# GLA level products of a diffusion block in column groups of 32 and 64 instead of full 128x128 matmuls

## The chip, the cores and the metric

The kernel runs on one core of a Trainium2 chip. The metric is the device time of one execution in microseconds (us). Engines: TensorE (PE; its weight loads are listed as PEld), VectorE (DVE), ScalarE (ACT), GpSimd (POOL) and SyncE (SP), which issues most DMAs.

## The reference

The block takes 256 latent tokens of width 2048 and 256 context tokens. After an RMSNorm with modulation comes one large projection, then two branches, retention and gated linear attention (GLA), each of 4 heads; their outputs are gated, merged and projected; a SwiGLU layer follows. What the change touches is the GLA branch, here for one head, in both directions:

```python
b = jnp.cumsum(ac, axis=2)                       # log decay, one per key channel (128)
decay = jnp.exp(b[:, :, :, None, :] - b[:, :, None, :, :])   # where i >= j (backward: the other half, exclusive)
scores = jnp.einsum('bhid,bhjd,bhijd->bhij', qc, kc, decay)
o = einsum('bhij,bhjv->bhiv', scores, vc) + einsum('bhid,bhdv->bhiv', qc * exp(b), s)
```

The decay depends on the query i, the key j and the channel d, so the 256x256 scores of a head are not one matmul. They have to be built for all pairs of tokens.

## The kernel before, in words

**Large matmuls.** Every weight block of 512 columns is streamed from HBM into `raw` (8 buffers), split by ScalarE into a rounded part `w_hi` (L643) and by VectorE into the rest `w_lo` (L1045), and multiplied by TensorE in three products for each pair of 128 rows (`products`, L1619, L1623, L1631): 12 float32r matmuls of 128x128 weights and 512 columns in a slot. ScalarE may split a slot only once TensorE has used the one four before it. This stream goes on through the whole kernel.

**The heads.** While TensorE computes the later columns of the input projection, the two branches are computed head by head between its slots. There is no planner: each engine has a list written out by hand, with a place p from 0 to 15 for each head. On TensorE `at_head(i, p)` (L1833) comes after the product slot of place p; on ScalarE and VectorE the steps of place p come before the split of that place. Each engine's list is in order, and semaphores tie them together.

**GLA scores by levels.** For a level h of 1, 2, 4, ..., 128, tokens are cut into blocks of 2h. A query in one half of a block and a key in the other half are compared through the middle of that block, so that the decay is a product of a query part and a key part. `exponents` (L1210) writes the two parts of the exponents for one level, for all 256 tokens, into `g_arg` (128 channels, 2, 4 levels, 256 tokens); ScalarE takes the exponential of four levels at once (L844); `weigh` (L1253) multiplies by queries and keys. Then TensorE multiplies keys by queries over the 128 channels (L1867): for levels 1 to 64 two 128x128 products, one for each half of 128 tokens; for level 128 two products that cross the halves. Levels 1, 2, 4, 8 are multiplied at p = 4, levels 16, 32, 64, 128 at p = 8, into banks 6 and 7 of PSUM. Of a 128x128 product only the pairs that belong to the level are wanted.

**Picking.** `g_a[:, 0:2, :]` starts as a diagonal matrix with the sum of q times k of each token (L1298). `pick` (L1261) then merges one level after another with a masked copy (L1273, 128 partitions by 256 elements, mask of 128x128 for each level), each waiting for the one before it. Near levels are picked at p = 5, ahead of the exponents of levels 16 to 128; far levels at p = 10. ScalarE copies the cross products of level 128 (L862). At p = 10 TensorE multiplies `g_a` by the values (L1887 to L1890).

**Beside it** the retention branch runs: transposes of its keys and queries at p = 3 and 6 (L1853, L1878), ScalarE's copies of them, behind the exponential of g_arg on its list (L856 r_qt, L858 r_kt), scores at p = 7 (L1896), the weighting by VectorE (L1309), outputs at p = 9 (L1912). GpSimd turns queries and keys by their position and issues the loads of the next head.

**A block of column groups** exists already elsewhere: L1801 sums 16 pieces of 512 columns with 32 columns of ones as weights, each in one of four groups of 32 columns of the array.

Of the kernel before, what the change touches and what calls it, by code (L numbers as in the profile page):

```python
# [10 lines left out]
U8 = mybir.dt.uint8  # L11
# [4 lines left out]
P = 128  # L16
D = 2048
KT = D // P
L = 256
# [30 lines left out]
def constants():  # L50

    f = np.float32
    n_f = RDK // 4
    inv = (f(10000.0) ** (-np.arange(n_f, dtype=f) / f(n_f))).astype(f)
    t = np.arange(L)
    ang = np.concatenate([(t // 64).astype(f)[:, None] * inv, (t % 64).astype(f)[:, None] * inv], axis=-1)
    rope = np.stack([np.cos(ang), np.sin(ang)], axis=1).astype(f)
    rope = rope.reshape(MT, P, 2, P).transpose(1, 2, 0, 3)
    s = np.arange(L)[:, None]
    i = np.arange(L)[None, :]  # L60
    delta = i - s
    dist = np.stack([np.maximum(delta, 0), np.maximum(-delta, 0), i + L - s, L - i + s], axis=0).astype(f)
    dist = dist.reshape(4, MT, P, L).transpose(2, 0, 1, 3)
    a, b = np.arange(P)[:, None], np.arange(P)[None, :]
    mask = np.stack([((a // h != b // h) & (a // (2 * h) == b // (2 * h))) for h in LEVELS[:-1]], axis=1)
    return {"k_ident": np.eye(P, dtype=f), "k_rope": np.ascontiguousarray(rope),
            "k_dist": np.ascontiguousarray(dist),
            "k_mask": np.ascontiguousarray(mask.astype(f))}


def build(nc, x, c, ctx_in, c_ctx, w_mod, b_mod, norm_mix_pre, norm_mix_post, norm_ffn_pre, norm_ffn_post,
# [10 lines left out]
    with ExitStack() as ctx:  # L82
# [5 lines left out]
        def keep(name, shape, dt=F32):  # L88

            size = math.prod(shape[1:]) * (4 if dt != mybir.dt.uint8 else 1)  # L90
            off = cursor[0]
            cursor[0] += (size + 31) // 32 * 32
            return at(name, shape, dt, off)
# [3 lines left out]
        def S(name):  # L97
            if name not in sems:
                sems[name] = ctx.enter_context(nc.semaphore(name))
            return sems[name]  # L100
# [21 lines left out]
        scale1 = keep("scale1", [P, 2, KT])  # L122
        mod2 = keep("mod2", [P, 2, KT])
        lg = keep("lg", [P, 2 * RH])
        mask = keep("mask", [P, 7, P], U8)
        spare = keep("spare", [P, 16])
        ssq = keep("ssq", [P, 4])
        rstd = keep("rstd", [P, 4])
# [11 lines left out]
        def reg(name, shape, kb, dt=F32):  # L140

            return at(name, shape, dt, base + kb * K)
# [4 lines left out]
        acc = reg("acc", [P, 4, D], 0)  # L147
        hc_hi = reg("hc_hi", [P, KT, L], 32, F32R)
        hc_lo = reg("hc_lo", [P, KT, L], 48, F32R)
        mask_f = reg("mask_f", [P, 7, P], 88)  # L150
        rows2 = reg("rows2", [96, P], 92)
        junk0 = reg("junk0", [P, D], 32)
        mod_row = reg("mod_row", [P, MOD_BLOCKS, N], 64)
# [277 lines left out]
        def _(pool):  # L431
# [15 lines left out]
            pool.dma_start(mask_f[:, :, :], k_mask).then_inc(S("consts_landed"), 16)  # L447
            pool.dma_start(ga_w[:, :, :], w_in_k[:, :, C_GA:C_GA + 2 * LOW]).then_inc(S("ga_landed"), 16)
            pool.dma_start(rope[:, :, :, :], k_rope).then_inc(S("tables_landed"), 16)
            pool.wait_ge(S("mask_ready"), 1)  # L450
            pool.memset(al_t[0][:, :], 1.0).then_inc(S("gate_rows_set"), 1)
            for r in (0, 64):
                for d in range(2):
# [585 lines left out]
        def _(dve):  # L1039
# [97 lines left out]
            for b in range(1, CTX_BLOCKS):  # L1137
                if b == 2:
                    dve.wait_ge(S("consts_landed"), 16 * 5)
                    dve.tensor_copy(mask[:, :, :], mask_f[:, :, :]).then_inc(S("mask_ready"), 1)  # L1140
                for j in range(8):
                    for n in chunks_at(b, j, 0):
                        add_chunk(0, n, *chunk_of(n))
                    split(S_CTX + 8 * b, j)
                    for n in chunks_at(b, j, 1):
                        add_chunk(0, n, *chunk_of(n))
# [102 lines left out]
            def hold(n):  # L1249

                dve.memset(spare[:, n:n + 1], 0.0)
# [6 lines left out]
                                             g_qkt[:, a:a + 1, :].broadcast_to([P, 4, L]), ALU.mult)  # L1258
                last.then_inc(S("g_qk_ready"), 1)

            def pick(i, r, n):  # L1261

                dve.wait_ge(S("g_levels_done"), i * 2 + (r + 1))
                if r == 1:
                    dve.wait_ge(S("g_cross_ready"), i + 1)
                for e in range(n):
                    if r == 1 or e > 0:
                        dve.wait_ge(S("g_picked"), i * 7 + (4 * r + e))
                    else:
                        dve.wait_ge(S("g_diag_ready"), i + 1)  # L1270
                    hold(4 * r + e)
                    src = bank(6, 2)[:, e * L:(e + 1) * L].rearrange("p (a n) -> p a n", a=2)
                    dve.copy_predicated(g_a[:, 0:2, :],  # L1273
                                        mask[:, 4 * r + e:4 * r + e + 1, :].broadcast_to([P, 2, P]), src)\
                        .then_inc(S("g_picked"), 1)

            dve.wait_ge(S("dctx_ready"), RH)
# [1 line left out]
            def head(i, final):  # L1279

                for p in range(16):
# [3 lines left out]
                    if p == 3:  # L1285
                        dve.wait_ge(S("g_st_exp"), i * 2 + 2)
                        dve.tensor_tensor(g_st[:, :, :], g_st[:, :, :], g_qkt[:, 0:1, :].broadcast_to([P, 2, L]), ALU.mult)\
                            .then_inc(S("g_st_ready"), 1)
                        dve.wait_ge(S("g_qk_landed"), i * 32 + 32)
                        dve.tensor_tensor(g_a[:, 0:2, :], g_q[:, :, :], g_k[:, :, :], ALU.mult)\  # L1290
                            .then_inc(S("g_diag_summed"), 1)
                        dve.wait_ge(S("g_diag_summed"), i * 2 + 1)
                        dve.tensor_reduce(spare[:, 12:12 + MT], g_a[:, 0:2, :], AX_X, ALU.add)\
                            .then_inc(S("g_diag_summed"), 1)
                        dve.wait_ge(S("g_diag_summed"), i * 2 + 2)
                        hold(9)
                        for m in range(MT):
                            last = dve.tensor_scalar(g_a[:, m, :], ident[:, :], spare[:, 12 + m:13 + m], GDK ** -0.5,  # L1298
                                                     ALU.mult, ALU.mult)
                        last.then_inc(S("g_diag_ready"), 1)  # L1300
                    if p == 5:
                        pick(i, 0, 4)
                        for e in range(4):
                            exponents(i, 4 + e)
                    if p == 7:
# [4 lines left out]
                                          dmat[:, bass.ds(i, 1), :, :].rearrange("p o a n -> p (o a) n"), ALU.mult)\  # L1310
                            .then_inc(S("r_a_ready"), 1)
                    if p == 10:
                        pick(i, 1, 3)

                        dve.wait_ge(S("r_o_done"), i + 1)
                        for m in range(MT):
                            dve.bn_stats(stats[:, 0, m, :], bank(4)[:, m * RDK:(m + 1) * RDK]).then_inc(S("r_stat"), 1)
                        dve.wait_ge(S("r_stat"), i * 4 + 2)
                        hold(8)
                        for m in range(MT):  # L1320
                            dve.bn_aggr(mv[:, 0, m, :], stats[:, 0, m, :]).then_inc(S("r_stat"), 1)
                        dve.wait_ge(S("r_stat"), i * 4 + 4)
                        dve.tensor_scalar(mv[:, 0, :, 1:2], mv[:, 0, :, 1:2], EPS, None, ALU.add)\
                            .then_inc(S("r_var_ready"), 1)
# [280 lines left out]
        def _(pe):  # L1605
# [227 lines left out]
            def at_head(i, p):  # L1833
# [15 lines left out]
                if p == 3:  # L1849
# [3 lines left out]
                            last = pe.transpose(bank(4)[:, f * L + m * P:f * L + (m + 1) * P],  # L1853
                                                r_kc[:, m, f * P:(f + 1) * P], ident[:, :])
                    last.then_inc(S("r_kc_turned"), 1)
                if p in (4, 8):
                    r = (p - 4) // 4
                    pe.wait_ge(S("g_qk_ready"), i * 2 + (r + 1))
                    if r == 0:
                        pe.wait_ge(S("g_s_ready"), i + 1)  # L1860
                    else:
                        pe.wait_ge(S("g_picked"), i * 7 + 4)
                    for e in range(4):
                        for m in range(MT):
                            key = m
                            qry = m if 4 * r + e < 7 else 1 - m
                            last = pe.matmul(bank(6, 2)[:, e * L + m * P:e * L + (m + 1) * P],  # L1867
                                             g_arg[:, 1, e, key * P:(key + 1) * P], g_arg[:, 0, e, qry * P:(qry + 1) * P],
                                             start=True, stop=True)
                    last.then_inc(S("g_levels_done"), 1)  # L1870
                if p == 6:
                    pe.wait_ge(S("rope_ready"), i * 4 + 4)
# [6 lines left out]
                                                    t[:, m, f * P:(f + 1) * P], ident[:, :])  # L1879
                    last.then_inc(S("r_qk_turned"), 1)  # L1880
                if p == 10:
                    pe.wait_ge(S("g_picked"), i * 7 + 7)
                    pe.wait_ge(S("g_cross_ready"), i + 1)
                    pe.wait_ge(S("g_st_ready"), i + 1)
                    for m in range(MT):
                        o, c = bank(6)[:, m * GDV:(m + 1) * GDV], slice(m * P, (m + 1) * P)
                        pe.matmul(o, g_a[:, m, :], g_v[:, 2 + m, :], start=True, stop=False)  # L1887
                        pe.matmul(o, g_a[:, 3 - m, :], g_v[:, 3 - m, :], start=False, stop=False)
                        pe.matmul(o, g_st[:, 0, c], g_s[:, 0, :], start=False, stop=False)
                        last = pe.matmul(o, g_st[:, 1, c], g_s[:, 1, :], start=False, stop=True)  # L1890
                    last.then_inc(S("g_o_done"), 1)
# [225 lines left out]
```

## Time and profile before

| | |
|---|---|
| median of 3 runs | 1728.86 us (1727.52 to 1730.07) |
| the profiled execution: time, span | 1727.43 us, 1725.7 us |
| TensorE busy | 1697.5 us, 98% |
| VectorE busy | 1010.8 us, 59% |
| ScalarE busy | 740.0 us, 43% |
| heads | from about 542 to 800 us |

The span is the time from the first to the last instruction of one profiled execution. Busy is the time in which an engine executed at least one instruction. A float32 matmul appears as two records of weight load and two of stream, a float32r matmul or a transpose as one of each. Streams are pipelined, so a record's length (275 ns for 128 columns) is more than the step from one to the next (109 ns).

### The profile page before, as it was taken

How to read it: one execution, taken by the hardware profiler on the slowest of the kernel's cores; microseconds unless marked ns; L12 is line 12 of the kernel's file. 1: busy time of each engine (PE TensorE's matmuls, PEld its weight loads, DVE VectorE, ACT ScalarE, POOL GpSimd, SP SyncE). 2: the span in 40 equal slices, each digit the busy share in tenths (PEclk: the TensorE clock that was granted, in tenths of full speed). 3: DMA queues.
4: the chain of work that ended last, by engine and by line, in shares of the span. 5: the costliest groups of instructions: out<-in, count | busy, mean ns of one | idle time of the engine just before them, and what ended most of it. 6: DMA issues, size and time to landing. Idle time of an engine off the chain costs nothing.

```text
span 1725.7 us, 21272 instructions
## 1 busy us (share of the span) xinstructions
PE 1697.5 (98%) x7805; PEld 1371.5 (79%) x7805; DVE 1010.8 (59%) x1145; ACT 740.0 (43%) x832; POOL 161.3 (9%) x179
## 2 busy tenths in 40 slices
PE   6999999999999999999999999999999999999998
PEld 2468888887878888888888788888888888888886
DVE  2446776648966677666665764444444545444444
ACT  3334222217555354455446564444444444443442
POOL 0011000000046245230000000000000000000000
PEclk9999999999999999999999999999999999999999
DMA  9999999968988666656776566666666666766652
GB/s 366 378 382 379 352 370 342 364 252 309 380 291 266 190 217 188 209 157 208 230 250 229 192 210 192 187 190 187 190 189 189 188 189 191 260 194 195 193 193 91
DMA packets 183708, 419.69 MB, mean 243 GB/s; under 512 B 12961, under 2 KB 13313, under 8 KB 173793
## 3 DMA queue, kind: packets, MB, share of 16 engines
q1 hardware_dynamic: 167680, 375.45, 65.7%
q0 software_dynamic: 7216, 28.07, 5.0%
q10 hardware_dynamic: 8752, 15.38, 2.4%
q8 instruction: 38, 0.62, 0.1%
q14 instruction: 22, 0.17, 0.0%
HBM read 398.35 MB, written 20.50 MB: 243 GB/s over the span
## 4 chain that ended last, share of the span: by engine, by line
PE 94%; DVE 2%; DMA 2%; issue 1%; ACT 1%; SPq 0%; POOL 0%; DVEq 0%; POOLq 0%; ACTq 0%
PE ps L1619 27%; PE ps L1623 27%; PE ps L1631 27%; PE ps L1701 2%; PE ps L1675 2%; DMA raw<-in_w_mod 2%; PE ps L1717 1%; PE ps L1896 1%; PE ps L1912 1%; PE ps L1950 1%; PE ps L1867 1%; PE ps L2028 0%; PE ps L1664 0%; PE ps L2015 0%; PE ps L2020 0%
## 5 line engine op out<-in xcount | busy, mean ns | idle before, releaser
L1045 DVE TENSOR_TENSOR w_lo<-raw,w_hi 128x1024 fp32r<-128x1024 f32 x486 | 600.5, 1238 | 509.2 <-ACT w_hi L643 508.9
L643 ACT ACTIVATE w_hi<-raw 128x1024 fp32r<-128x1024 f32 x488 | 515.9, 1060 | 781.1 <-PE ps L1631 764.7
L1619 PE MATMUL ps<-w_hi,h_hi 128*128 128x512 f32 x1440 | 452.7, 395 | 0.0
L1623 PE MATMUL ps<-w_hi,h_lo 128*128 128x512 f32 x1440 | 445.3, 390 | 0.0
L1631 PE MATMUL ps<-w_lo,h_hi 128*128 128x512 f32 x1440 | 392.6, 389 | 0.0
L1623 PEld LDWEIGHTS ps<-w_hi,h_lo 128*128 128x128 f32 x1440 | 270.4, 188 | 56.7
L1631 PEld LDWEIGHTS ps<-w_lo,h_hi 128*128 128x128 f32 x1440 | 270.3, 188 | 56.3
L1619 PEld LDWEIGHTS ps<-w_hi,h_hi 128*128 128x128 f32 x1440 | 266.9, 188 | 55.1 <-ACT w_hi L643 1.5
L1057 DVE SCALAR_TENSOR_TENSOR acc<-wm,csil,acc 128x2048 f32<-128x2048 f32 x60 | 140.9, 2349 | 57.8 <-DMA wm<-in_w_mod 57.6
L1619 PE MATMUL ps<-w_hi,hid_hi 128*128 128x512 f32 x352 | 109.8, 390 | 0.0
L1623 PE MATMUL ps<-w_hi,hid_lo 128*128 128x512 f32 x352 | 109.7, 389 | 0.0
L1631 PE MATMUL ps<-w_lo,hid_hi 128*128 128x512 f32 x352 | 94.8, 389 | 0.0
L1631 PEld LDWEIGHTS ps<-w_lo,hid_hi 128*128 128x128 f32 x352 | 66.1, 188 | 13.7
L1623 PEld LDWEIGHTS ps<-w_hi,hid_lo 128*128 128x128 f32 x352 | 66.1, 188 | 13.7
L1619 PEld LDWEIGHTS ps<-w_hi,hid_hi 128*128 128x128 f32 x352 | 66.0, 188 | 13.6
L1623 PE MATMUL ps<-w_hi,hc_lo 128*128 128x512 f32 x192 | 59.1, 389 | 0.0
L1619 PE MATMUL ps<-w_hi,hc_hi 128*128 128x512 f32 x192 | 59.1, 389 | 0.0
L1631 PE MATMUL ps<-w_lo,hc_hi 128*128 128x512 f32 x192 | 57.8, 389 | 0.0
L1675 PE MATMUL ps<-raw,c_pad 128*32 128x512 f32 x256 | 45.3, 617 | 8.1 <-DMA raw<-in_w_mod 6.2
L623 POOL DMA_DIRECT2D hs<-hsd x1 | 0.7, 718 | 479.1 <-DVE hid_n L1565 479.1
L1107 DVE TENSOR_TENSOR w_lo<-raw,w_hi 128x1024 fp32r<-128x1024 f32 x16 | 19.3, 1223 | 44.3 <-ACT w_hi L716 44.3
L1623 PEld LDWEIGHTS ps<-w_hi,hc_lo 128*128 128x128 f32 x192 | 36.1, 188 | 7.5
(308 smaller groups left out, 1407.4 us busy)
## 6 DMA issues: line engine op xcount, KB each, us to landing
raw<-in_w_in SPq DMA_DIRECT2D x184, 512.0 KB, 6.3
wm<-in_w_mod SPq DMA_DIRECT2D x64, 1024.0 KB, 7.0
raw<-in_ffn_w_gate SPq DMA_DIRECT2D x88, 512.0 KB, 4.5
raw<-in_ffn_w_up SPq DMA_DIRECT2D x88, 512.0 KB, 4.4
raw<-in_ffn_w_down SPq DMA_DIRECT2D x88, 512.0 KB, 4.6
raw<-in_w_mod SPq DMA_DIRECT2D x64, 512.0 KB, 8.1
raw<-in_w_out SPq DMA_DIRECT2D x32, 512.0 KB, 4.7
px<-stage ACTq DMA_DIRECT2D x44, 256.0 KB, 6.0
```

The costliest lines, as they stand in the source:

```text
L643: act.activation(w_hi[:, j % SPLIT, :, :], raw[:, j % RAW, :, :], ACT.Copy).then_inc(w_high, 1)
L1045: dve.tensor_tensor(w_lo[:, j % SPLIT, :, :], raw[:, j % RAW, :, :], w_hi[:, j % SPLIT, :, :].bitcast(F32), ALU.subtract).then_inc(w_low, 1)
L1057: dve.scalar_tensor_tensor(out=a, in0=wm[:, b, :], scalar=csil[:, k:k + 1], in1=a, op0=ALU.mult, op1=ALU.add).then_inc(S("wm_used"), 1)
L1107: dve.tensor_tensor(w_lo[:, o % SPLIT, :, :], raw[:, place % RAW, :, :], w_hi[:, o % SPLIT, :, :].bitcast(F32), ALU.subtract)\
L1619: pe.matmul(o, hi[:, kk, c], w_h[:, e, :], start=kk == 0, stop=False)
L1623: pe.matmul(o, lo[:, kk, c], w_h[:, e, :], start=False, stop=False)
L1631: last = pe.matmul(o, hi[:, kk, c], w_l[:, e, :], start=False, stop=kk == last_k)
L1675: last = pe.matmul(bank(6)[g * GROUP:(g + 1) * GROUP, :], c_pad[:, k, :], raw[:, place % RAW, e, :], start=k < 4, stop=k >= KT - 4, tile_p ...
L1701: last = pe.matmul(bank(n), t[:, 2 * i + e, m * P:(m + 1) * P], w[:, q, e, :], start=i == 0 and r == 0 and a == 0, stop=i == 7 and r == 2 ...
L1717: last = pe.matmul(bank(4 + m), t[:, 2 * i + e, m * P:(m + 1) * P], w[:, q, e, :], start=i == 0 and a == 0, stop=i == 7 and a == 5)
L1867: last = pe.matmul(bank(6, 2)[:, e * L + m * P:e * L + (m + 1) * P], g_arg[:, 1, e, key * P:(key + 1) * P], g_arg[:, 0, e, qry * P:(qry + ...
L1896: last = pe.matmul(bank(4, 2)[:, a * L:(a + 1) * L], r_kt[:, 2 * (a // 2) + f, (a % 2) * P:(a % 2 + 1) * P], r_qt[:, f, :], start=f == 0, ...
```

## The change

The near levels (1, 2, 4, 8) only pair tokens inside groups of 32. They are now multiplied in four column groups: 32 keys by the same 32 queries, four levels, two halves and four groups, 32 matmuls into bank 6, in 256 columns. Level 16 stays inside groups of 32 too, level 32 pairs a group with its neighbour, level 64 in two groups of 64; level 128 stays as it was. These are 2 + 8 + 8 + 4 = 22 matmuls at p = 8.

The picking of near levels is done in 32 columns (`g_near`, 128x2x32), on top of a diagonal of 32 columns. The far products fill the whole 128x128 block of each half in bank 6: level 16 the diagonal 32x32 blocks, level 32 the blocks next to them, level 64 the off-diagonal 64x64 blocks. `pick_far` copies all of it to `g_a` and then puts `g_near` over the diagonal, where key and query lie in the same 16 tokens (mask 4), in one masked copy for each group of 32 partitions. Its wait for `g_cross_ready` goes; TensorE still waits for that at p = 10. The diff below has the details; the mask constant shrinks from 7x128 to 6x32 columns.

```diff
-    a, b = np.arange(P)[:, None], np.arange(P)[None, :]
-    mask = np.stack([((a // h != b // h) & (a // (2 * h) == b // (2 * h))) for h in LEVELS[:-1]], axis=1)
+    a, b = np.arange(P)[:, None] % GROUP, np.arange(GROUP)[None, :]
+    mask = np.stack([((a // h != b // h) & (a // (2 * h) == b // (2 * h))) for h in LEVELS[:4]]
+                    + [a // LEVELS[4] == b // LEVELS[4], a == b], axis=1)
...
+            def pick_near(i):
+
+                dve.wait_ge(S("g_levels_done"), i * 2 + 1)
+                for e in range(4):
+                    if e > 0:
+                        dve.wait_ge(S("g_picked"), i * 9 + e)
                     else:
                         dve.wait_ge(S("g_diag_ready"), i + 1)
+                    hold(e)
+                    src = bank(6)[:, e * MT * GROUP:(e + 1) * MT * GROUP].rearrange("p (m n) -> p m n", m=MT)
+                    dve.copy_predicated(g_near[:, :, :], mask[:, e:e + 1, :].broadcast_to([P, MT, GROUP]), src)\
+                        .then_inc(S("g_picked"), 1)
+
+            def pick_far(i):
+
+                dve.wait_ge(S("g_levels_done"), i * 2 + 2)
+                dve.wait_ge(S("g_diag_summed"), i * 2 + 2)
+                dve.tensor_copy(g_a[:, 0:2, :], bank(6)[:, 0:L].rearrange("p (m n) -> p m n", m=MT)).then_inc(S("g_picked"), 1)
+                dve.wait_ge(S("g_picked"), i * 9 + 5)
+                hold(4)
+                for g in range(4):
+                    r = slice(g * GROUP, (g + 1) * GROUP)
+                    dve.copy_predicated(g_a[r, 0:2, r], mask[r, 4:5, :].broadcast_to([GROUP, MT, GROUP]), g_near[r, :, :])\
                         .then_inc(S("g_picked"), 1)
...
-                            last = dve.tensor_scalar(g_a[:, m, :], ident[:, :], spare[:, 12 + m:13 + m], GDK ** -0.5,
+                            last = dve.tensor_scalar(g_near[:, m, :], ident_g[:, :], spare[:, 12 + m:13 + m], GDK ** -0.5,
                                                      ALU.mult, ALU.mult)
...
+                if p == 4:
+                    pe.wait_ge(S("g_qk_ready"), i * 2 + 1)
+                    pe.wait_ge(S("g_s_ready"), i + 1)
                     for e in range(4):
                         for m in range(MT):
+                            for g in range(4):
+                                c = slice(m * P + g * GROUP, m * P + (g + 1) * GROUP)
+                                o = (e * MT + m) * GROUP
+                                last = pe.matmul(bank(6)[g * GROUP:(g + 1) * GROUP, o:o + GROUP], g_arg[:, 1, e, c],
+                                                 g_arg[:, 0, e, c], start=True, stop=True, tile_position=(0, g * GROUP))
+                    last.then_inc(S("g_levels_done"), 1)
+                if p == 8:
+                    pe.wait_ge(S("g_qk_ready"), i * 2 + 2)
+                    pe.wait_ge(S("g_picked"), i * 9 + 4)
+                    for m in range(MT):
+                        pe.matmul(bank(7)[:, L + m * P:L + (m + 1) * P], g_arg[:, 1, 3, m * P:(m + 1) * P],
+                                  g_arg[:, 0, 3, (1 - m) * P:(2 - m) * P], start=True, stop=True)
+                    for e, w, far in ((0, GROUP, 0), (1, GROUP, 1), (2, 2 * GROUP, 1)):
+                        for m in range(MT):
+                            for g in range(P // w):
+                                k, q = m * P + g * w, m * P + (g ^ far) * w
+                                last = pe.matmul(bank(6)[g * w:(g + 1) * w, q:q + w], g_arg[:, 1, e, k:k + w],
+                                                 g_arg[:, 0, e, q:q + w], start=True, stop=True, tile_position=(0, g * w))
                     last.then_inc(S("g_levels_done"), 1)
```

## Rows read from the trace of the kernel before

**Rows 1.** The page: busy time by engine, granted clock, chain by engine.
```profile
PE 1697.5 (98%) x7805; PEld 1371.5 (79%) x7805; DVE 1010.8 (59%) x1145; ACT 740.0 (43%) x832; POOL 161.3 (9%) x179
...
PEclk9999999999999999999999999999999999999999
...
PE 94%; DVE 2%; DMA 2%; issue 1%; ACT 1%; SPq 0%; POOL 0%; DVEq 0%; POOLq 0%; ACTq 0%
```
**Rows 2.** Waits of TensorE: line waited for, us, times, longest.
```profile
PE ps L1896 <- ACT r_kt L858: 1.2, 1, 1.2
...
PE ps L1701 <- DVE w_lo L1107: 1.0, 1, 1.0
```
**Rows 3.** Chain of waits, head two: start us, us, what.
```profile
623.16 0.92 PE ps L1631 x4
624.08 1.78 PE ps L1867 x16
```
**Rows 4.** TensorE in order of time around L1801, two narrow windows: start us, us.
```profile
490.34 0.39 PE L1631 MATMUL ps<-w_lo,h_hi 128*128 128x512 f32 x1
490.66 0.64 PE L1801 MATMUL ps<-acc,ones 128*32 128x512 f32 x4
...
493.69 0.61 PE L1801 MATMUL ps<-acc,ones 128*32 128x512 f32 x4
494.23 0.50 PE L1619 MATMUL ps<-w_hi,h_hi 128*128 128x512 f32 x1
```
**Rows 5.** Weight loads in order of time, same stretch; [idle before].
```profile
490.66 0.16 PEld L1801 LDWEIGHTS ps<-acc,ones 128*32 128x32 f32 x8 [0.35 <-issue]
491.12 0.13 PEld L1801 LDWEIGHTS ps<-acc,ones 128*32 128x32 f32 x4 [0.30 <-issue]
...
493.26 0.13 PEld L1801 LDWEIGHTS ps<-acc,ones 128*32 128x32 f32 x4 [0.30 <-issue]
```
**Rows 6.** Line L1801.
```profile
L1801 PE MATMUL ps<-acc,ones x32: 592/592/617, 490.7 to 493.7; 128*32 128x512 f32 x32
```
**Rows 7.** VectorE's groups by form, 540 to 830: busy us, mean ns | idle.
```profile
L1224 DVE TENSOR_TENSOR g_arg<-cum 128x128 f32 x24 | 6.8, 284 | 0.0
...
L1232 DVE TENSOR_TENSOR g_st<-cum 128x256 f32 x3 | 1.2, 414 | 0.0
```
**Rows 8.** VectorE in order of time, head two, place 5.
```profile
626.44 0.44 DVE L1273 COPY_PREDICATED g_a<-mask,ps 128x256 f32<-128x256 uint8 x1
...
627.89 0.44 DVE L1273 COPY_PREDICATED g_a<-mask,ps 128x256 f32<-128x256 uint8 x1
...
628.23 0.28 DVE L1223 TENSOR_TENSOR g_arg<-cum 128x128 f32 x1
628.42 0.28 DVE L1224 TENSOR_TENSOR g_arg<-cum 128x128 f32 x1
```
**Rows 9.** VectorE's last far merge and TensorE's outputs, head two.
```profile
648.91 0.44 DVE L1273 COPY_PREDICATED g_a<-mask,ps 128x256 f32<-128x256 uint8 x1
...
651.69 0.38 PE L1887 MATMUL ps<-g_v,g_a 128*128 128x256 f32 x1
```
**Rows 10.** ScalarE and TensorE in order of time, heads one and two.
```profile
571.93 0.59 ACT L858 ACTIVATE r_kt<-ps 128x512 f32<-128x512 f32 x1
572.57 0.48 PE L1896 MATMUL ps<-r_qt,r_kt 128*128 128x256 f32 x1 [1.20 <-ACT r_kt L858]
...
623.92 1.95 PE L1867 MATMUL ps<-g_arg 128*128 128x128 f32 x16
...
631.57 1.92 ACT L844 ACTIVATE g_arg<-g_arg 128x2048 f32<-128x2048 f32 x1 [1.88 <-DVE g_arg L1226]
...
633.87 0.59 ACT L858 ACTIVATE r_kt<-ps 128x512 f32<-128x512 f32 x1
...
634.80 1.46 PE L1896 MATMUL ps<-r_qt,r_kt 128*128 128x256 f32 x6
```
**Rows 11.** Line L1140, the mask's cast.
```profile
L1140 DVE CAST mask<-mask_f x1: 617/617/617, 161.0 to 161.0; 128x896 uint8<-128x896 f32 x1
```

More of the change, by code:

```diff
@@ L124, in build @@
         lg = keep("lg", [P, 2 * RH])
-        mask = keep("mask", [P, 7, P], U8)
+        mask = keep("mask", [P, 5, GROUP], U8)
+        ident_g = keep("ident_g", [P, GROUP])
+        g_near = keep("g_near", [P, MT, GROUP])
         spare = keep("spare", [P, 16])
@@ L149, in build @@
         hc_lo = reg("hc_lo", [P, KT, L], 48, F32R)
-        mask_f = reg("mask_f", [P, 7, P], 88)
+        mask_f = reg("mask_f", [P, 6, GROUP], 88)
         rows2 = reg("rows2", [96, P], 92)
@@ L449, in _ @@
             pool.dma_start(rope[:, :, :, :], k_rope).then_inc(S("tables_landed"), 16)
-            pool.wait_ge(S("mask_ready"), 1)
+            pool.wait_ge(S("mask_ready"), 2)
             pool.memset(al_t[0][:, :], 1.0).then_inc(S("gate_rows_set"), 1)
@@ L1139, in _ @@
                     dve.wait_ge(S("consts_landed"), 16 * 5)
-                    dve.tensor_copy(mask[:, :, :], mask_f[:, :, :]).then_inc(S("mask_ready"), 1)
+                    dve.tensor_copy(mask[:, :, :], mask_f[:, 0:5, :]).then_inc(S("mask_ready"), 1)
+                    dve.tensor_copy(ident_g[:, :], mask_f[:, 5, :]).then_inc(S("mask_ready"), 1)
                 for j in range(8):
@@ L1259, in weigh @@
                 last.then_inc(S("g_qk_ready"), 1)
[L1261 to L1268, printed above, removed]
+            def pick_near(i):
[3 more added lines that the diff above has]
+                        dve.wait_ge(S("g_picked"), i * 9 + e)
                     else:
                         dve.wait_ge(S("g_diag_ready"), i + 1)
[L1271 to L1274, printed above, removed]
+                    hold(e)
[11 more added lines that the diff above has]
+                    dve.copy_predicated(g_a[r, 0:2, r], mask[r, 4:5, :].broadcast_to([GROUP, MT, GROUP]), g_near[r, :, :])\
                         .then_inc(S("g_picked"), 1)
@@ L1301, in head @@
                     if p == 5:
-                        pick(i, 0, 4)
+                        pick_near(i)
                         for e in range(4):
@@ L1312, in head @@
                     if p == 10:
-                        pick(i, 1, 3)
+                        pick_far(i)
                         dve.wait_ge(S("r_o_done"), i + 1)
@@ L1855, in at_head @@
                     last.then_inc(S("r_kc_turned"), 1)
[L1856 to L1862, printed above, removed]
+                if p == 4:
+                    pe.wait_ge(S("g_qk_ready"), i * 2 + 1)
+                    pe.wait_ge(S("g_s_ready"), i + 1)
@@ L1863, in at_head @@
                     for e in range(4):
                         for m in range(MT):
[L1865 to L1869, printed above, removed]
+                            for g in range(4):
[3 more added lines that the diff above has]
+                                                 g_arg[:, 0, e, c], start=True, stop=True, tile_position=(0, g * GROUP))
@@ L1881, in at_head @@
                 if p == 10:
-                    pe.wait_ge(S("g_picked"), i * 7 + 7)
+                    pe.wait_ge(S("g_picked"), i * 9 + 9)
                     pe.wait_ge(S("g_cross_ready"), i + 1)
```

## The prediction

> **What bounds the kernel now.** I read the page first. TensorE is busy 98% of the span, at a granted clock of full speed in all forty slices, and the chain that ended last is 94% TensorE [rows 1]. So time taken off TensorE's queue comes off the end, as long as no other engine is then late. The waits of TensorE in the stretch of the four heads tell how many places there are where it already waits: one, 1.2 us, in the first head, at the retention scores (L1896), for ScalarE's copy of r_kt [rows 2]. In heads two to four it never waits; the row counts one time.
>
> **The level products before.** Each of the eight blocks (two in each head) is 8 float32 matmuls, and each of these is two records of load and two of stream, so 16 of each kind. A block takes 1.78 us in the chain [rows 3], some 110 ns a record.
>
> **What a column-group block costs.** One block in the trace is built as the new ones: L1801, 16 float32 matmuls of 32 columns of weights in four groups, 512 wide. Its last batch is four streams of 592 ns that all fit into 0.61 us, so they start some 7 ns apart [rows 4]. The loads come in fours every 0.43 us ((493.26 - 491.12)/5) [rows 5]: four 512-wide records run in the time of one. The whole block has 8 batches, 3.42 us. The last product matmul before it starts at 490.34; the first after it starts at 494.23 and lasts 0.50 instead of 0.39, so it is really under way at 494.34 [rows 4]. That is 4.00 us; less 0.23 for the ordinary step between two product matmuls (0.92 us for four [rows 3]) it is 3.77. Entering and leaving the mode therefore costs 3.77 - 3.42 = 0.35 us: a pause ahead of it, a pause behind it, and the first weight loads, which nothing hides.
> The Trainium skill states, in TensorEngine Tiling (Array Packing), section Key Properties, that changing the tiling mode drains the engine. The loads' idle time of 0.35 us before the block agrees [rows 5].
>
> **Part 1, near levels (p = 4).** Removed: 16 records, 1.78 us. Added: 32 matmuls, 64 records, in 16 batches of four groups. With b for the time of a batch, the block costs 0.35 + 16b. Bounds of b: at least 27 ns, the 512-wide batch's 427 ns scaled to 32 columns; at most 436 ns, if each small record took the 109 ns of a 128-wide one and none overlapped. A batch of 512 columns takes 427 to 429 ns, so hardly more than its stream; loads in a burst start 7 ns apart (eight in 0.16 us, each 0.11 [rows 5]), which makes 28 ns for four. I take b = 33 ns, near the bottom, because four starts, one load and one stream each need 27 or 28 ns and overlap in the row that has this form. Near block: 0.35 + 0.53 = 0.88 us, 0.90 us less than now; by the bounds 1.00 less or 5.5 more.
>
> **Part 2, far levels (p = 8).** Removed: 1.78 us. Added: two full matmuls across the halves (4 records, 0.44 us), then 16 matmuls of 32 columns (8 batches, 8b = 0.26), then 4 of 64 columns in two groups (4 batches; 64 columns stream in 53 ns, with 3 ns between: 0.22). The mode is entered, changed once from 32 to 64, and left: 0.35 and about 0.15 more for the second pause and load (the half of the overhead that lies ahead of L1801's first stream is 0.32 us from start to start [rows 4], less the last stream's 0.21, plus load: 25 ns for 32 columns, 617 against 592 [rows 6], and twice that for 64). Sum 1.42 us, 0.36 less than now. Bounds: with b = 27, 0.41 less; with every record at 109 ns, 3.5 us more.
>
> **Part 3, VectorE.** Seven merges of 128x256 at 0.44 us in each head [rows 8] become four of 64 columns, one plain copy of 256 and four of 32 partitions by 64. The four near ones step by 0.48 to 0.49 us ((627.89 - 626.44)/3 [rows 8]): 0.44 and some 0.045 of handshake. No row has a masked copy of 64 columns. Bounds: 0.20 us, the step of the exponent operations of 128 columns [rows 8], and 0.49, no gain. Between 128 and 256 columns the elementwise operations from SBUF go from 284 to 414 ns (L1224, L1232 [rows 7]), 1 ns a column, so 192 columns fewer give 0.25, a step of 0.29; I take that. Four near merges then save 0.80 us of VectorE. The diagonal, two operations of 128 columns at about 0.28, becomes two of 32, but two splits lie between it and the merges, which wait for ScalarE and it for TensorE, so in heads two to four nothing is counted; all of it could not bring more than 0.2 us. The far side is about even (three at 0.49 against about 0.4 and four at about 0.2) and its consumer, TensorE at p = 10, starts at 651.69 while the merges end at 649.35 [rows 9]: 2.3 us of cover; were the far copies each as dear as now, 2.4 us in all instead of 1.46, 1.4 us of it would still be left.
>
> **What is late next.** Near merges, exponents of levels 4 to 7, ScalarE's exponential, its copies of r_qt and r_kt, and then L1896 form one row of work: in head two the merges start at 626.44, the exponential at 631.57, r_kt ends at 633.87 + 0.59 = 634.46, and L1896 starts at 634.80 [rows 8, 10]. Its start trails a release by 0.05 us (572.52 to 572.57 in head one [rows 10]), and then shows its first load of about 0.1 us unhidden (0.48 against 0.38 for a stream of this width [rows 9, 10]), so the real cover is 0.34 - 0.15, about 0.19 us. Before the merges VectorE is not freed by anything in part 1, as it reaches them at 626.44, after the block's last record (623.92 + 1.95 [rows 10]). So TensorE gets to L1896 0.90 us earlier, and r_kt is there 0.80 us earlier with 0.19 us of cover: the gain in heads two to four may be up to 0.99 us, and 0.90 fits, barely. In head one TensorE already waits, so there the gain is what the row of VectorE gains, 0.80, and about 0.05 of the diagonal.
>
> **Part 4, constants.** The mask goes from 128x896 to 128x192 columns; its cast takes 617 ns once, at 161 us [rows 11], and of TensorE's waits only one of 1.0 us lies between the opening and the heads, and that (L1701) is of the opening's last products [rows 2]. The wait of GpSimd for it is the second of two casts instead of the first; behind it are loads used some 230 us later. I cost it at nothing; were the cover gone it would be some 0.3 us of gain.
>
> **Sum.** Near: 3 x 0.90 + 0.85 = 3.55. Far: 4 x 0.36 = 1.44. Together 5.0 us. The profiled execution took 1727.43 us for a span of 1725.7; it would take 1722.4. The median of the runs is 1728.86, so 1723.9 as a median.
>
> **Rivals.**
> One stream at a time. At 32 columns the groups don't run side by side, and each record takes its own stream of 27 ns in turn, with the load hidden. Then near is 0.35 + 64 x 0.027 = 2.08 (0.30 more than now), far 0.44 + 0.50 + 32 x 0.027 + 8 x 0.053 = 2.22 (0.44 more); three heads lose 0.74 each, the first 0.44 - 0.85, and the time is 1730.7. For it: no block in the trace runs more than four records in 0.43 us. Against it: bursts at 7 ns a record [rows 4, 5].
> The Trainium skill has a rule to this end in TensorE: Matmul & The Clock Gate, section "Wait — 56ns, not 53.3ns?": start to start never drops below about 25 ns however small the matmul. By its figure the time would be about 1730; by the bursts on L1801 it would not hold across column groups.
> The merges don't shrink. If a masked copy keeps its 0.49 us, L1896 holds TensorE in every head: heads two to four keep 0.19 each of the near gain and head one 0.05, with 1.44 of the far blocks: 2.1 us, 1726.8. For it: fixed costs of PSUM reads; against it the 1 ns a column.
> Slower: load and stream hide nothing, and one record runs at a time. A record of 32 columns needs 27 ns of load (25 seen above) and 27 of stream. If each stream is over before the next load is there, a record costs 54 ns: near 0.35 + 3.46 = 3.81 (2.03 more), far 0.44 + 0.50 + 32 x 0.054 + 8 x 0.107 (64 columns, twice both) = 3.53 (1.75 more). Three heads lose 3.78, head one loses 1.75 and 2.03 - 1.2, which the present wait swallows: 13.9 us, 1742.8. At 109 ns a record it would be 35 us. It decides from 22 ns a record on: there the eight blocks together lose what head one gains; from 31 ns on it is more than 0.2%. Against it stands only the 512-wide row, in which a load has 400 ns to hide behind.
>
> **How the numbers follow.** The forecast's case 0.58, with its own range 1722.3 to 1725.4 (b from 27 to 52 ns); one stream at a time 0.15; merges don't shrink 0.14; slower 0.11, of which most lies beyond 0.2%; 0.02 for more gain than I can name. A change of 0.2%, 3.5 us, is about what runs of this kernel tell from none. Faster by more: 0.58 and 0.02, so 0.6. Within: 0.15, 0.14 and a little, 0.3. Slower: 0.1. The range leaves out the slow case and the best few per cent: 1722.2 to 1731.
>
> **What would show it.** The near block's chain piece, 1.78 now, at about 0.9 with 64 records and fours of loads every 0.03 us; over 1.8 one of the two serial cases holds. The far block at about 1.4, with two drains in it. Near merges at about 250 ns. TensorE's wait at L1896: about 1.2 to 1.3 us in head one, and in heads two to four none or under 0.1; waits of half a microsecond there mean the merges did not shrink. The forecast is wrong if a batch of four takes over 52 ns, or if TensorE waits elsewhere in the heads.

## The result, and the profile after

The changed kernel takes 1739.02 us (median of 6 runs, 1737.83 to 1741.83) against 1728.06 us (6 runs, 1727.34 to 1730.07) for the one before: ratio 1.0063, 95% interval 1.0053 to 1.0073. It is 11 us slower where 5 us less were forecast, and the time lies outside the range given. Its profiled execution took 1737.88 us for a span of 1736.2 us.

The steps that the prediction worked out are where it put them. The chain of waits of the changed kernel, head two (start us, us, what), against [rows 3]:

```profile
629.74 0.69 PE ps L1877 x50
630.43 0.66 PE ps L1632 x2
...
645.93 0.45 PE ps L1884 x4
646.38 0.77 PE ps L1890 x40
647.14 0.66 PE ps L1632 x2
```

The near block and what it leaves on the next two products is 0.69 + 0.66 - 0.47 = 0.88 us (0.47 is such a pair elsewhere), forecast 0.88. The far block is 0.45 + 0.77 + 0.19 = 1.41 us, forecast 1.42. The loads of the near block, against [rows 5]:

```profile
629.67 0.65 PEld L1877 LDWEIGHTS ps<-g_arg 128*32 128x32 f32 x64 [0.35 <-issue]
```

64 loads start within 0.65 us, sixteen batches of four, the last of them 0.11 us long: some 34 ns from one batch to the next, under 9 ns a record. VectorE in order of time, near merges and far side of head two, against [rows 8, 9]:

```profile
632.02 0.23 DVE L1275 COPY_PREDICATED g_near<-mask,ps 128x64 f32<-128x64 uint8 x1
632.04 0.06 DVE L1255 MEMSET spare<- 128x1 f32 x1
632.29 0.23 DVE L1275 COPY_PREDICATED g_near<-mask,ps 128x64 f32<-128x64 uint8 x1
...
652.36 0.42 DVE L1282 COPY g_a<-ps 128x256 f32<-128x256 f32 x1
652.82 0.22 DVE L1287 COPY_PREDICATED g_a<-mask,g_near 32x64 f32<-32x64 uint8 x1
652.85 0.06 DVE L1255 MEMSET spare<- 128x1 f32 x1
653.07 0.74 DVE L1287 COPY_PREDICATED g_a<-mask,g_near 32x64 f32<-32x64 uint8 x3
```

A near merge steps by 0.27 us (forecast 0.29). TensorE's waits in the stretch of the heads are still a single one, as in [rows 2]:

```profile
PE ps L1918 <- ACT r_kt L861: 1.2, 1, 1.2
```

So the time was lost elsewhere, and by no wait: TensorE is busy for 98% of a longer span, at full clock. The groups by line name the place. Page of the kernel before (busy us, mean ns | idle), products of the down projection and of the projection of the context:

```profile
L1619 PE MATMUL ps<-w_hi,hid_hi 128*128 128x512 f32 x352 | 109.8, 390 | 0.0
...
L1619 PE MATMUL ps<-w_hi,hc_hi 128*128 128x512 f32 x192 | 59.1, 389 | 0.0
```

The same groups on the page after:

```profile
L1632 PE MATMUL ps<-w_hi,hid_hi 128*128 128x512 f32 x352 | 111.7, 395 | 0.0
...
L1632 PE MATMUL ps<-w_hi,hc_hi 128*128 128x512 f32 x192 | 61.5, 402 | 0.0
```

Products that the change does not touch have become longer. How many of them fit into a fixed stretch tells the step from one to the next. Three stretches (columns: stretch, its us, TensorE busy and its records (x), granted clock, DMA share, GB/s): the projection of the context, the down projection, and 400 to 480 us, where only `h_hi` and `h_lo` are weights. Kernel before:

```profile
100.00:380.00 280.00, 279.00 (x1252) 1.00 0.96 355
1500.00:1700.00 200.00, 200.00 (x884) 1.00 0.59 186
...
400.00:480.00 80.00, 80.00 (x361) 1.00 1.00 371
```

and after:

```profile
100.00:380.00 280.00, 279.06 (x1225) 1.00 0.97 354
1500.00:1700.00 200.00, 200.00 (x862) 1.00 0.61 194
...
400.00:480.00 80.00, 80.00 (x360) 1.00 0.95 347
```

In the down stage 200/884 = 226 ns a product became 200/862 = 232. From start to start of every record there it is 226.7 and 232.4 ns, 5.7 ns more. Between 400 and 480 us the count is 360 instead of 361, so next to nothing has changed. By stage, from the first record of one to the first of the next: the context's 336.2 to 342.6 us, output and up projections 673.2 to 675.3, down 240.0 to 246.0, together 14.5 us more. The down stage has 3 x 352 products, 1056 x 5.7 ns = 6.0 us; the output projection has 384 with `o_hi` and `o_lo` as weights, which step by 5.5 ns more, 2.1 us. In the context stage the 576 products with `hc` (3 x 192) step by 234.1 ns instead of 226.6, and the 480 products of `h` that alternate with them by 230.6 instead of 226.7: 4.3 + 1.8 us. So products of `h` are slower there too, though neither `h` nor the streamed tiles have moved. What the heads save is in the first and last start of two lines, before and after:

```profile
L1801 PE MATMUL ps<-acc,ones x32: 592/592/617, 490.7 to 493.7; 128*32 128x512 f32 x32
L1619 PE MATMUL ps<-w_hi,o_hi x128: 387/389/477, 804.8 to 893.0; 128*128 128x512 f32 x128
```

```profile
L1814 PE MATMUL ps<-acc,ones x32: 592/593/617, 497.3 to 500.3; 128*32 128x512 f32 x32
L1632 PE MATMUL ps<-w_hi,o_hi x128: 390/393/479, 807.2 to 897.4; 128*128 128x512 f32 x128
```

804.8 - 490.7 = 314.1 us became 807.2 - 497.3 = 309.9: 4.2 us less. 14.5 - 4.2 = 10.3, and the spans differ by 1736.2 - 1725.7 = 10.5.

**What hid, hc and o have in common.** `keep` places the lasting tiles one behind the other; `base` is the next multiple of 128 bytes, and the tiles made with `reg`, among them `hc_hi`, `hc_lo`, `o_hi`, `o_lo`, `hid_hi`, `hid_lo`, lie whole KB behind `base`. `raw`, `w_hi`, `w_lo`, `h_hi`, `h_lo` are placed ahead of the mask and did not move. The mask gave up 736 bytes, `ident_g` and `g_near` took 384, and `base` went from byte 134016 to 133632 of each partition. Modulo 256 that is from 128 to 0; `w_hi`, `w_lo`, `h_hi` and `h_lo` lie at 128. The theory tested below: a product step depends on how the tile that serves as weights and the streamed tile lie to each other.

### The profile page after: what moved, and what is told of

Same layout as the page of the kernel before. It is cut to its first block, busy times and chain, and to the rows that moved or that the text cites. A ratio compares the mean times of both kernels' runs of the same rounds, so it can differ in the third digit from the quotient of the medians.

```text
span 1736.2 us, 21875 instructions
## 1 busy us (share of the span) xinstructions
PE 1708.4 (98%) x8109; PEld 1365.4 (79%) x8109; DVE 1007.6 (58%) x1146; ACT 740.2 (43%) x832; POOL 164.4 (9%) x179
## 4 chain that ended last, share of the span: by engine, by line
PE 95%; DVE 2%; DMA 1%; issue 1%; ACT 1%; POOL 0%; DVEq 0%; SPq 0%; POOLq 0%; ACTq 0%
PE ps L1632 27%; PE ps L1644 27%; PE ps L1636 27%; PE ps L1714 2%; PE ps L1688 2%; DMA raw<-in_w_mod 1%; PE ps L1730 1%; PE ps L1918 1%; PE ps L1934 1%; PE ps L1972 1%; PE ps L2050 0%; PE ps L1677 0%; PE ps L2037 0%; PE ps L2042 0%; DVE xr_t L422 0%
## 5 line engine op out<-in xcount | busy, mean ns | idle before, releaser
L1632 PEld LDWEIGHTS ps<-w_hi,hc_hi 128*128 128x128 f32 x192 | 36.4, 190 | 8.1
```

The source lines that it names most:

```text
L1632: pe.matmul(o, hi[:, kk, c], w_h[:, e, :], start=kk == 0, stop=False)
```

## The experiments

In these, a "step" is the mean time from the start of one product to the start of the next, over consecutive products with the weights named.

**e1 and e2: only the tiles behind the constants are moved.** e1 is the changed kernel with 384 unused bytes:

```diff
-        base = (cursor[0] + 127) // 128 * 128
+        base = (cursor[0] + 127) // 128 * 128 + 384
```

e2 is the kernel before with three small tiles packed into one, so that `base` falls to 133888, a multiple of 256:

```diff
-        ssq = keep("ssq", [P, 4])
-        rstd = keep("rstd", [P, 4])
-        minus_half = keep("minus_half", [P, 4])
+        small = keep("small", [P, 12])
```

> The changed kernel, with all tiles behind the constants (base) put back to the byte where they stood before: 384 bytes of padding, nothing else. Placement theory: the change of the level products is worth the 4 to 5 us forecast, and the loss comes only from tiles that moved by 384 bytes because the mask shrank; product steps in the context, up and down stages go back from 232.4 ns to 226.8, and the time is 1723 to 1724.5 us. Rival (the column-group blocks or the longer program slow TensorE): nothing changes, 1738 to 1740, with 232.4 ns steps.

> The kernel before with its old level products; three small tiles are packed so that base comes to lie 128 bytes lower, on a multiple of 256 bytes (133888). Placement theory with a period of 256: product steps of 232.4 ns in the context, up and down stages and 1741 to 1744 us. If the period is 512 bytes, so that 133888 (256 beyond a multiple of 512) is harmless: 1728. Rival (blocks or program): 1728, steps of 226.8.

Measured: e1 1723.97 us (9 runs, 1722.81 to 1726.13), ratio to before 0.9976, interval 0.9967 to 0.9986. e2 1744.02 us (1742.74 to 1744.49), ratio 1.0091, 1.0076 to 1.0107. Windows of e1 and then of e2:

```profile
100.00:380.00 280.00, 278.99 (x1252) 1.00 0.97 353
1500.00:1700.00 200.00, 200.00 (x884) 1.00 0.60 184
```

```profile
100.00:380.00 280.00, 279.06 (x1225) 1.00 0.96 348
1500.00:1700.00 200.00, 200.00 (x862) 1.00 0.62 198
```

e2 has nothing of the change and the counts of the changed kernel; e1 has all of it and the counts of the kernel before. The loss is the placement and nothing else. Without it the change brings 4.1 us. That is by the medians: the profiled execution of e1 has a span only 2.1 us shorter than that of the kernel before (1723.6 against 1725.7), because it reached L1801 1.3 us later (491.96 instead of 490.66) and took 1.5 us longer behind the heads (922.4 from the first product of `o_hi` to the end instead of 920.9). e3 below, the same kernel with `base` 256 bytes lower, saves as much in the heads and has 920.9 behind them, so those 1.5 us do not come from the change.

**e3 and e4: how far apart.** As e1, with 128 and with 64 bytes instead of 384 (`base` 133760 and 133696).

> The changed kernel with base 128 bytes up (133760, as far beyond a multiple of 512 as the tiles raw, w_hi and h_hi are). Placement theory: steps of 226.8 ns or less everywhere, 1723 to 1725 us. Rival: 1738 to 1740.

> The changed kernel with base 64 bytes up (133696). Placement theory leaves the size open: if only a multiple of 256 is dear, steps of 226.8 ns and 1723 to 1725 us; if what counts is whether a row of weights begins on the same place in 128 bytes as the streamed tile, steps differ from both. Rival: 1738 to 1740.

Measured, one run each, kernel before on that chip 1727.97: e3 1723.8, e4 1734.34. At 128 beyond a multiple of 256 the time is the good one. At 64 the products of `o` and `hid` step by 228.9 ns, some 2 ns more than good and not 5.6, and the context's stretch holds 1232 products, most of the way from 1252 to 1225.

**e5 and e6: absolute or relative?** e5 puts 128 bytes ahead of `raw` and `base` at 133888, so that streamed tiles, `h` and all weights lie at multiples of 256. e6 leaves the weights at 128 and moves only `w_hi` and `w_lo` to 0 (128 bytes ahead of `w_hi`, 128 ahead of `h_hi`).

```diff
+        cursor[0] += 128
         raw = keep("raw", [P, RAW, 2, N])
...
-        base = (cursor[0] + 127) // 128 * 128
+        base = 133888
```

> The changed kernel with everything moved by half of 256 bytes: 128 bytes of padding ahead of raw, and base at 133888, so that the streamed tiles (w_hi, w_lo) and all weights (h, hc, o, hid) begin a row on a multiple of 256 bytes. If the place of the weights alone counts: steps of 232.4 ns in every stage, about 1723.9 + 5000 records x 5.7 ns more for h, so 1752 to 1765 us. If it counts whether weights and streamed tile lie alike in 256 bytes: steps of 226.8 everywhere, 1722 to 1726.

> The changed kernel with all weights where they are harmless (128 beyond a multiple of 256, base 134016), and only the streamed tiles w_hi and w_lo moved onto a multiple of 256. Weights' place alone: 226.8 ns everywhere, 1722 to 1726. Likeness of the two: 232.4 everywhere, 1752 to 1765.

Measured, one run each, kernel before there 1728.05: e5 1721.21 (a little under what was expected; e9 times it again), e6 1756.32, 28 us slower than before. Windows of e6 (in the second only products of `h`):

```profile
100.00:380.00 280.00, 279.13 (x1228) 1.00 0.97 354
400.00:480.00 80.00, 80.00 (x352) 1.00 0.95 342
1500.00:1700.00 200.00, 200.00 (x866) 1.00 0.63 204
```

Now the products of `h` step by 232.4 ns too, though `h` has not been moved, only the streamed tile. The address itself doesn't matter; how the two lie to each other does.

**e7 and e8: other distances.** `base` at 96 and at 192 beyond a multiple of 256, `hid_lo` 64 and 96 bytes further on, that is at 160 and at 32.

> The changed kernel with base 96 bytes beyond a multiple of 256, and hid_lo 64 bytes further, at 160. So far 0 gave steps of 232.4 ns, 64 gave 228.9 (down stage), 128 gave 226.7. If the cost falls in equal measure towards 128, 96 and 160 give some 227.8; if only 128 is free and everything else costs by its distance from 0, the same; a rule by 64-byte pieces would leave 96 at 226.7 or at 228.9. Time 1724 to 1732.

> The same with base at 192 and hid_lo at 32 beyond a multiple of 256. Symmetry about 128 would give 228.9 at 192 and some 230.6 at 32; 1728 to 1737 us. If 192 is free, 226.7 for hid_hi.

Measured, one run each: 1737.73 and 1738.45, both above the range expected. The table has the weights' place less the streamed tile's, modulo 256, and the step among the products of the output projection, where `o_hi` and `o_lo` lie at one and the same distance:

| distance | 0 | 128 | -64 | +64 | -32 |
|---|---|---|---|---|---|
| step, ns | 226.8 | 232.4 | 228.9 | 233.3 | 233.3 |
| seen in | before, e1, e5 | after, e2, e6 | e4 | e8 | e7 |

In the down stage of e7 and e8 `hid_lo` (+32 and -96) alternates with `hid_hi` (-32 and +64). From one product of `hid_lo` to the next the step is 229.2 and 231.7 ns there, which is no clean value for those distances, since the context stage shows that neighbours change a product's step.

Only equal places give 226.8. The rest is neither even nor symmetric, and no rule for it was found. The single steps behind these means show more. Between 1500 and 1700 us they stay at 225 to 228 ns in the kernel before. In the changed kernel they repeat every seven products, 241, 232, 231, 232, 228, 230, 233 ns, with mean 232.4, whichever of `hid_hi` and `hid_lo` is loaded; in e4 they repeat every three, 226, 229, 232. So unequal places do not add one fixed delay to each product: some steps are about as short as before and the others longer, in a fixed rhythm.

**e9: is 0 better than 128?** The kernel of e5 again, timed.

> The changed kernel with 128 unused bytes ahead of raw and 256 behind the constants, so that the streamed tiles and the weights that are multiplied with them all begin at multiples of 256 bytes. Theory (only the likeness modulo 256 bytes counts, 0 is as good as 128): product steps of 226.8 ns in every stage and the time of the version that was moved back by 384 bytes, 1724.0, within 1.5 us of it; the single look at 1721.2 then was scatter of one run. Rival (multiples of 256 are better in themselves): the time stays near 1721.2, 2.5 us and more below it, with some stage shorter than there.

Measured: 1723.3 us (6 runs, 1720.75 to 1725.02), before 1728.49 on that chip, ratio 0.9967, 0.9955 to 0.9979. This overlaps with e1's interval. The count in the down stage is e1's 884 again. It is the fastest version measured, by no more than the intervals allow.

**e10 and e11: the two halves of the change.** Both are e1 with one of the two blocks multiplied by 8 full matmuls as in the kernel before: in e10 the far levels, in e11 the near ones. e10's edit:

```diff
-                    for e, w, far in ((0, GROUP, 0), (1, GROUP, 1), (2, 2 * GROUP, 1)):
...
+                            qry = m if e < 3 else 1 - m
+                            last = pe.matmul(bank(6, 2)[:, e * L + m * P:e * L + (m + 1) * P],
+                                             g_arg[:, 1, e, m * P:(m + 1) * P], g_arg[:, 0, e, qry * P:(qry + 1) * P],
+                                             start=True, stop=True)
```

> The changed kernel moved back by 384 bytes, with the far levels multiplied by eight full 128-column matmuls as before, but picked as in the changed kernel, so the far levels of the output aren't the reference's. What is left is the gain of the near levels. Theory (the forecast's terms hold): each far block is back at 1.78 us in the chain, 0.36 us longer, so 1.44 us over the version with both, 1725.4; against the kernel before 3.55 us less (1724.5 by the forecast's sum), so 1724.5 to 1725.4. Rival (the near gain is swallowed at the retention scores, which then hold TensorE in heads two to four): a wait of 0.3 us or more there and 1726.5 or more.

> The changed kernel moved back by 384 bytes, with the near levels multiplied by eight full 128-column matmuls as before, but picked in 32 columns as in the changed kernel, so the near levels of the output aren't the reference's. What is left is the gain of the far levels and of the shorter merges. Theory: near blocks 1.78 us, TensorE's one wait at the retention scores in head one falls from 1.2 to some 0.4 us and gives 0.8, the far blocks give 4 x 0.36 = 1.44, together 2.3 us: 1725.8 against 1728.06. Rival (the column groups of 64 and the change of width cost more than the chain shows): 1727 or more.

Measured: e10 1725.54 us (11 runs), ratio 0.9984, 0.9975 to 0.9993; e11 1726.77 us (11 runs), ratio 0.9992, 0.9983 to 1.0001, which alone is not told from no change. e11 lies 1 us above the 1725.8 expected, close to the 1727 of its rival; the chain tells which of the terms held. From the first L1801 to the first product of `o_hi`, starts of e1, e10, e11:

```profile
L1814 PE MATMUL ps<-acc,ones x32: 592/592/617, 492.0 to 495.0; 128*32 128x512 f32 x32
L1632 PE MATMUL ps<-w_hi,o_hi x128: 387/389/476, 801.2 to 889.4; 128*128 128x512 f32 x128
```

```profile
L1814 PE MATMUL ps<-acc,ones x32: 592/592/617, 492.2 to 495.3; 128*32 128x512 f32 x32
L1632 PE MATMUL ps<-w_hi,o_hi x128: 387/389/476, 802.9 to 891.1; 128*128 128x512 f32 x128
```

```profile
L1814 PE MATMUL ps<-acc,ones x32: 592/592/617, 492.6 to 495.7; 128*32 128x512 f32 x32
L1632 PE MATMUL ps<-w_hi,o_hi x128: 387/389/476, 804.9 to 893.0; 128*128 128x512 f32 x128
```

309.2, 310.7 and 312.3 us against 314.1 before: the whole saves 4.9, near alone 3.4 (forecast 3.55), far alone 1.8. Both halves contain the 0.4 us that the shorter merges save in head one (below), so they add up to 0.3 us more than the whole. In e11 the far blocks and the shorter merges were expected to bring 2.3; the chain shows the far block as forecast, but TensorE's wait in head one fell to 0.8 us and not to 0.4:

```profile
PE ps L1917 <- ACT r_kt L861: 0.8, 1, 0.8
```

That is 1.44 + 0.4 = 1.8. The merges of head one do take 0.74 us less (1.05 from the first to the exponents, 1.79 before), but they begin 4.46 us after the start of the near block and not 4.13 (566.77 - 562.31 against 564.49 - 560.36), which takes 0.33 back. Why VectorE comes to them later is left open.

**e12: how close VectorE was.** e1 with each near merge done twice, the second time into an unused tile:

```diff
+                    dve.copy_predicated(g_dup[:, :, :], mask[:, e:e + 1, :].broadcast_to([P, MT, GROUP]), src)
                     dve.copy_predicated(g_near[:, :, :], mask[:, e:e + 1, :].broadcast_to([P, MT, GROUP]), src)\
```

> The changed kernel moved back by 384 bytes, with each of the four near merges of a head done a second time into an unused tile; nothing else differs. It tests how near the row of VectorE was to the retention scores. Theory (the forecast: 0.8 us saved there and 0.9 on TensorE just about match, with 0.1 to 0.2 us of cover): four merges more are 0.9 to 1.1 us, so TensorE waits 0.7 to 0.9 us at the retention scores in heads two to four, where it waited for nothing, and 0.9 to 1.1 us more in head one: 3.0 to 3.8 us over the version without, 1727.0 to 1727.8. Rival (there is more cover than reckoned, and the merges need not have shrunk): only head one shows it, 1725.0.

Measured: 1724.37 us (11 runs), ratio 0.998, 0.9971 to 0.9989. The time is nearer to the rival's, the trace is not: from the first L1801 (now L1817, 491.1 us) to the first product of `o_hi` (801.8) it is 310.7 us, 1.5 more than in e1, and not 3.0 to 3.8. VectorE and TensorE in head two, and TensorE's wait in the heads:

```profile
626.01 0.22 DVE L1277 COPY_PREDICATED g_dup<-mask,ps 128x64 f32<-128x64 uint8 x1
626.03 0.06 DVE L1257 MEMSET spare<- 128x1 f32 x1
626.14 0.22 DVE L1278 COPY_PREDICATED g_near<-mask,ps 128x64 f32<-128x64 uint8 x1
626.41 0.23 DVE L1277 COPY_PREDICATED g_dup<-mask,ps 128x64 f32<-128x64 uint8 x1
```

```profile
632.81 0.91 PE ps L1647 x4
633.76 3.72 PE ps L1921 x16
```

```profile
PE ps L1921 <- ACT r_kt L863: 1.7, 1, 1.7
```

Two merges step by 0.40, only 0.13 more than one, since the second need not wait for the first's semaphore. Four bring 0.52 us and not 1. Of these TensorE loses 3.72 - 3.45 = 0.27 (e1's piece there is 3.45) and a pause of 0.04, 0.31 us in all, in head two, and 0.4 in head one. The cover was thus 0.52 - 0.31 = 0.2 us. The mechanism of the forecast holds, since every head pays; its size as expected for this run was wrong, because a merge without its wait costs half. By the same reckoning, as an estimate, merges as long as before ([rows 8], 0.49 and not 0.27, so 0.88 us more) would have cost the heads 0.88 - 0.2 = 0.7 us each.

## Why the prediction was wrong

**Right.** What bounds the kernel: TensorE's queue, and time off it comes off the end. A batch of four (33 ns taken, 34 seen), the near block (0.88), the far block (1.42, 1.41 seen), the merges' step (0.29, 0.27 seen), one wait in the heads. The sum of 5.0 us is 4.9 in e1 by the two starts. That the median of e1, 1723.97, also meets the 1723.9 forecast is in part luck: the forecast counted down from 1728.86, while the kernel before took 1727.97 beside e1, so the medians differ by 4.0 us (0.0014 to 0.0033 of the time, 2.4 to 5.7 us). Of the rivals, one stream at a time and one record at a time are excluded by 64 loads in 0.65 us; that the merges don't shrink, by 0.23 us of length. By the rule of the Trainium skill that was weighed (TensorE: Matmul & The Clock Gate, section "Wait — 56ns, not 53.3ns?", no start to start below about 25 ns) the block would have cost, as an estimate, 64 x 25 ns at least, 1.6 us; across column groups this trace shows 64 loads in 0.65 us and 64 streams in 0.76.

**Wrong: "Part 4, constants ... I cost it at nothing."** That part counted the mask's cast and the waits for it, its time, and not its bytes. The tile's size decides where all later tiles lie. The chain is: mask 896 to 160 bytes, two new tiles of 128 and 256, `base` 384 bytes earlier, weights and streamed tile no longer at equal places modulo 256, some 5.6 ns more a product of `o` and `hid`, 7.5 a product of `hc` and 3.8 a product of `h` between those. It costs 14.5 us by stage, which swallows the 4.2 us that the heads gain. Each link has its run: e2 for the placement without the change, e1 and e3 for the change without the placement, e6 for the streamed tile's side, e5 for the address alone. Nothing in the rows of before could have priced it, as all products stood at equal places there; but the code shows that `base` moves, and a line of the forecast should have said that the weights of 2016 products (576, 384, 1056) change address (and of 96 more at the end of the opening), with an unknown cost. No rival had its place outside the heads.

0.7 us of the heads' gain is missing in the changed kernel (4.2 against 4.9 in e1). e2 shows that this is the placement too: it has the level products of before, and the same two starts lie 813.0 - 498.2 = 314.8 us apart, 0.7 more than in the kernel before.

```profile
L1800 PE MATMUL ps<-acc,ones x32: 592/592/617, 498.2 to 501.2; 128*32 128x512 f32 x32
L1618 PE MATMUL ps<-w_hi,o_hi x128: 390/393/479, 813.0 to 903.2; 128*128 128x512 f32 x128
```

The steps between products of `h` in that stretch are longer by 0.6 to 0.7 ns on average (227.8 in the kernel before and in e1, 228.5 in the changed kernel, 228.3 in e2), over some 940 of them. Which of the moved tiles does this was not tried.

What makes TensorE slower at unequal places is not shown. Weight loads and streams overlap in time ([rows 1]: 79% and 98% of the span), and a conflict between the two reads would fit e6; but no run separates that from another cause. Nor does the finding reach beyond the float32r products of 512 columns: the transposes at p = 6 (`ident` and `r_q`) stand at unequal places in the changed kernel too, and their piece in the chain of head two is 0.87 us before and after:

```profile
631.32 0.87 PE ps L1878 x8
```

```profile
636.12 0.87 PE ps L1900 x8
```

The Trainium skill (SBUF — State Buffer, section Operand start alignment) gives the rule for legal start addresses and says of it that it is about legality and not speed; the runs here add the speed.

## What to carry to other kernels

A change to a small tile is a change to the place of every tile allocated behind it: print the addresses before and after, and hold large operands still with an explicit offset, or the measurement is of two changes. Where a kernel is nothing but matmuls, place the weights and the streamed operand at equal offsets modulo 256 bytes; and if busy time per record rises in lines that nobody edited while waits stay, look at addresses first. Then the column groups are worth having: with the placement restored this change is 0.24% faster (0.0014 to 0.0033 of the time), and with everything at multiples of 256, 0.33%.

## What the runs showed of the hardware

The mean step of a float32r product of 128x128 weights and 512 columns lies between 226.8 and 233.3 ns with the operands' distance modulo 256 bytes, at the same granted clock of 1.00. At unequal distances the single steps run through a cycle, 228 to 241 ns every seven products at 128, 226 to 232 every three at -64. Where `hc` at distance 128 and `h` at distance 0 alternate as weights, both are slower, 234.1 and 230.6 ns. A distance of 256 is as good as none (e3 and e1 differ by 256 bytes, with 884 records each in the same 200 us), one of 128 is not. Small float32 matmuls in four column groups start a load about every 9 ns (64 in 0.65 us). A masked copy of 64 columns that waits for the one before it starts 0.27 us after it, one that doesn't wait 0.13 us after, so about half of the step of a short chained merge goes with its wait.
